# The gate and up tiles of a SwiGLU FFN multiplied in pairs by seven half products (a Strassen step) in an fp32 encoder trunk

## The reference, cut to what matters

```python
def swiglu(x, w_gate, w_up, w_down):        # x 512x1024, gate and up 1024x2816, down 2816x1024
    return (jax.nn.silu(x @ w_gate) * (x @ w_up)) @ w_down

for i in range(DEPTH):                      # 4
    ...                                     # h = mixer(x): convolution, spatial gating, short convolution, convolution
    x = layer_norm(ALPHA * x + h, ln1_g[i], ln1_b[i])
    x = layer_norm(ALPHA * x + swiglu(x, ffn_w_gate[i], ffn_w_up[i], ffn_w_down[i]), ln2_g[i], ln2_b[i])
    gate = jax.nn.sigmoid(x @ ple_w_gate[i])
    x = x + gate * rms_norm(p[i] @ ple_w_proj[i], ple_norm_g[i])
```

## Time and profile before

| | |
|---|---|
| time, three runs | 2602.64, 2599.68, 2602.08 us, median 2602.08 us |
| the profiled execution | span 2597.9 us from first to last instruction; the page gives no device time of its own for it, the median of the runs is 4.2 us above the span |
| instructions | 34084, of them 14649 matmuls |
| busy, share of the span | TensorE matmuls 99%, VectorE 55%, ScalarE 40%, GpSimd 0% |
| transfers | 239.63 MB, mean 92 GB/s |

### The profile page before, as it was taken

One profiled execution on the slowest core, in us unless ns is written; L12 is line 12 of the kernel. 1 busy time (PEld: TensorE's weight loads), 2 busy tenths in 40 slices (PEclk: granted clock), 3 DMA queues, 4 the chain that ended last, 5 costly groups with the idle time before them and its releaser, 6 DMA issues.

```text
span 2597.9 us, 34084 instructions
## 1 busy us (share of the span) xinstructions
PE 2574.2 (99%) x14649; PEld 2235.0 (86%) x14649; DVE 1421.1 (55%) x1639; ACT 1049.3 (40%) x1692; POOL 1.4 (0%) x10
## 2 busy tenths in 40 slices
PE   9999999999999999999999999999999999999999
PEld 7999888889888898888898898888898999888888
DVE  7978333277454663333784473333677977333276
ACT  6765222226233252222362253222356765222235
POOL 0000000000000000000000000000000000000000
PEclk9999999999999999999999999999999999999999
DMA  5203333324222223333232323333322113333322
GB/s 161 66 26 98 97 97 97 99 88 130 89 98 89 82 90 97 97 98 106 82 98 97 98 74 110 95 97 104 97 90 97 60 36 94 98 96 97 99 84 79
DMA packets 193290, 239.63 MB, mean 92 GB/s; under 512 B 14908, under 2 KB 139124, under 8 KB 193012
## 3 DMA queue, kind: packets, MB, share of 16 engines
q1 hardware_dynamic: 192564, 236.94, 28.8%
q10 hardware_dynamic: 576, 0.52, 0.1%
HBM read 233.21 MB, written 2.10 MB: 91 GB/s over the span
## 4 chain that ended last, share of the span: by engine, by line
PE 91%; DVE 7%; ACT 1%; issue 0%; DMA 0%; SPq 0%; DVEq 0%
PE psum L782 16%; PE psum L781 16%; PE psum L783 16%; PE psum L926 13%; PE psum L799 6%; PE psum L801 6%; PE psum L800 6%; PE psum L840 3%; PE psum L771 2%; PE psum L772 2%; PE psum L777 2%; DVE w_lo L1587 1%; DVE xf L1817 1%; DVE xf L1837 1%; DVE rstd L1829 1%; PE psum L1103 1%
## 5 line engine op out<-in xcount | busy, mean ns | idle before, releaser
L1587 DVE TENSOR_TENSOR w_lo<-raw,w_hi 128x1024 fp32r<-128x1024 f32 x431 | 517.9, 1222 | 566.2 <-ACT w_hi L1175 565.2
L1175 ACT CAST w_hi<-raw 128x1024 fp32r<-128x1024 f32 x431 | 445.1, 1048 | 673.2 <-DMA raw<-in_ffn_w_up_dram 331.8
L781 PE MATMUL psum<-a_hi,w_lo 128*128 128x512 f32 x928 | 361.4, 389 | 0.0
L783 PE MATMUL psum<-a_hi,w_hi 128*128 128x512 f32 x928 | 361.2, 389 | 0.0
L782 PE MATMUL psum<-a_lo,w_hi 128*128 128x512 f32 x896 | 348.8, 389 | 0.0
L781 PE MATMUL psum<-h_hi,w_lo 128*128 128x512 f32 x872 | 341.6, 392 | 0.0
L783 PE MATMUL psum<-h_hi,w_hi 128*128 128x512 f32 x872 | 339.6, 389 | 0.0
L782 PE MATMUL psum<-h_lo,w_hi 128*128 128x512 f32 x856 | 333.4, 389 | 0.0
L926 PE MATMUL psum<-a_hi,w_lo 128*128 128x256 f32 x1088 | 280.1, 286 | 6.7 <-DVE w_lo L1587 5.1
L926 PE MATMUL psum<-a_hi,w_hi 128*128 128x256 f32 x1088 | 276.6, 283 | 0.0
L926 PEld LDWEIGHTS psum<-a_hi,w_lo 128*128 128x128 f32 x1088 | 208.7, 192 | 8.7 <-DVE w_lo L1587 4.6
(11 more groups left out here) (299 smaller groups left out, 4053.9 us busy)
## 6 DMA issues: line engine op xcount, KB each, us to landing
raw<-in_ffn_w_gate_dram SPq DMA_DIRECT2D x176, 256.0 KB, 2.8
raw<-in_ffn_w_up_dram SPq DMA_DIRECT2D x176, 256.0 KB, 3.1
raw<-in_ffn_w_down_dram SPq DMA_DIRECT2D x176, 256.0 KB, 2.8
raw<-in_a_w_pw_dram SPq DMA_DIRECT2D x94, 256.0 KB, 2.9
raw<-in_ple_w_gate_dram SPq DMA_DIRECT2D x64, 256.0 KB, 2.7
raw<-in_b_w_in_dram SPq DMA_DIRECT2D x64, 256.0 KB, 2.9
raw<-in_c_w_in_dram SPq DMA_DIRECT2D x48, 256.0 KB, 2.9
raw<-in_b_w_out_dram SPq DMA_DIRECT2D x32, 256.0 KB, 2.7
```

Source lines behind the costliest of these rows:

```text
L781: pe.matmul(bank(grp.g, j), st_lo, mv_hi, start=(k == 0), stop=False, skip_group_check=by_tiles(grp))
L783: done = pe.matmul(bank(grp.g, j), st_hi, mv_hi, start=False, stop=(ku == last and a == UK - 1), skip_group_check=by_tiles(grp))
L1175: act.copy(hi_u[u % RING], raw_u[u % RING]).then_inc(hi_ready, 1)
L1587: dve.tensor_tensor(lo_u[u % RING], raw_u[u % RING], hi_u[u % RING].bitcast(F32), ALU.subtract)\
```

## The change

From the third group on, the FFN's gate and up product runs in a new stage, `ffn_pairs`, of 18 groups a layer. A pair is one gate tile and one up tile (128 features each). Gate and up are the two block rows, the lower and the upper half of the 1024 input features the two block columns of a 2 x 2 block matrix; tokens 0 to 255 and 256 to 511 are the two block columns of x. Seven products of half size (128 features x 512 input features x 256 tokens) take the place of eight. Each product lands in its own half bank, seven of the eight half banks of a PSUM half.

- A pair has two units. A unit holds four k-tiles of one gate and one up tile (`load_pair`), in runs of 128 columns (512 B) where before they were of 256 columns (1 KB); its bytes are as before.
- Per unit VectorE forms four sums of weight blocks (one add of 512 columns, two of 256, each on the one before), ScalarE casts three plain blocks (768 columns) and the four sums (1024), VectorE subtracts 768 and 1024 columns (`pair_hi`, `pair_lo`). Their work space is the w_hi slots and, for every third unit, other buffers: three units' worth (`work_freed`).
- Per layer four sums of x blocks are formed and split (`sum_tokens`, `sum_lo`).
- TensorE issues 7 x 2 x 3 = 42 matmuls of 256 columns a unit (`pair`).
- Behind a pair ScalarE copies one half bank (`pairs_first`), VectorE makes four additions of half banks, placed between the steps of a later unit's `pair_lo`, ScalarE takes silu in SBUF (`pairs_gate`), VectorE multiplies (`pair_product`).
- The hidden tiles of the pairs are cast and subtracted in the down projection (`hidden_split`, `hidden_lo`), since the x sums lie in their place until then. The down projection's first six casts wait until their w_hi slots are free of pair work (`hi_freed`).

```diff
+PLAIN = 2
+PAIRS = D_FF // P - 2 * PLAIN
+PAIR_UNITS = 2
+SPLIT_AT = 2 * PLAIN
+WORK = 3
...
-        stage("ffn_in", layer, DT, FT // 2)
+        stage("ffn_in", layer, DT, PLAIN)
+        stage("ffn_pairs", layer, DT, PAIRS)
...
+        def pair_slots(u):
+            s, n = pair_unit(u)
+            first = s.groups[0].unit
+            if n % WORK == 0:
+                return mean_var[:, 0:3 * HALF], tiles(h_hi, SPLIT_AT, 2), sums_lo[:, :], tiles(tmp, 4, 2)
+            slots = [(first + WORK * (n % WORK - 1) + i) % RING for i in range(WORK)]
+            return hi_u[slots[0]][:, 0:3 * HALF], hi_u[slots[1]], hi_u[slots[2]], hi_f32[slots[2]]
...
+        def work_freed(u):
+            s, n = pair_unit(u)
+            if n >= WORK:
+                return pe_done, used[u - WORK]
+            return pe_done, used[s.groups[0].unit - (RING - WORK + 1, 1)[n - 1]]
+        def hi_freed(u):
+            for s in stages:
+                if s.kind == "ffn_pairs" and 0 <= u - s.groups[-1].unit - PAIR_UNITS < RING:
+                    end = s.groups[-1].unit + PAIR_UNITS
+                    return pe_done, used[end - (2 if u - end < WORK else 1)]
+            return None
...
+            def load_pair(s, grp, ku):
+                u, f = grp.unit + ku, SPLIT_AT + grp.index
+                sp.wait_ge(*slot_freed(u))
+                dst = raw_u[u % RING].rearrange("p (i k n) -> p i k n", i=2, k=TILES)
+                for i, name in enumerate(("ffn_w_gate", "ffn_w_up")):
+                    view = ins[name][s.layer].rearrange("(k e p) n -> p e k n", e=PAIR_UNITS, p=P)
+                    sp.dma_start(dst[:, i], view[:, ku, :, f * P:(f + 1) * P])\
+                      .then_inc(raw_landed[u % RING], 16)
...
+            def pair(s, grp):
+                if grp.index == 0:
+                    pe.wait_ge(token_lo, TILES * (s.layer + 1))
+                take_half(grp.g)
+                for ku in range(PAIR_UNITS):
+                    u = grp.unit + ku
+                    pe.wait_ge(pair_x_lo, pair_count(u))
+                    pe.wait_ge(*lo_of_unit(u))
+                    x_hi, s_hi, s_lo, _ = pair_slots(u)
+                    x_lo = lo_u[u % RING][:, HALF:4 * HALF]
+                    own = lambda i: (piece(x_hi, i), piece(x_lo, i))
+                    added = lambda i: (piece(s_hi, i), piece(s_lo, i))
+                    for at, w, y in ((0, own(1), (0, 0)), (2, own(2), (1, 0)), (3, added(2), 2), (5, added(0), 0),
+                                     (6, added(1), 1), (1, added(3), (1, 1)), (4, own(0), 3)):
+                        o = piece(bank(grp.g, 0, TILES), at)
+                        for a in range(UK):
+                            k = ku + PAIR_UNITS * a
+                            w_hi_k, w_lo_k = (x[:, a * P:(a + 1) * P] for x in w)
+                            if isinstance(y, int):
+                                y_hi, y_lo = (piece(x, k) for x in token_sum(y))
+                            else:
+                                y_hi, y_lo = (hcol(tiles(x, TILES * y[0] + k), y[1]) for x in (a_hi, a_lo))
+                            first = k == 0 and at in (0, 2, 5, 6)
+                            pe.matmul(o, w_lo_k, y_hi, start=first, stop=False, skip_group_check=True)
+                            pe.matmul(o, w_hi_k, y_lo, start=False, stop=False, skip_group_check=True)
+                            done = pe.matmul(o, w_hi_k, y_hi, start=False, stop=(ku == PAIR_UNITS - 1 and a == UK - 1),
+                                             skip_group_check=True)
+                        if at == 4 if ku == 0 else at in (3, 6, 1, 4):
+                            done.then_inc(pe_done, 1)
...
+                if hi_freed(u):
+                    act.wait_ge(*hi_freed(u))
                 act.copy(hi_u[u % RING], raw_u[u % RING]).then_inc(hi_ready, 1)
             split_end = [0]
+            def pair_hi(u):
+                x_hi, s_hi, _, sums = pair_slots(u)
+                act.wait_ge(raw_landed[u % RING], 32 * (u // RING + 1))
+                if pair_unit(u)[1]:
+                    act.wait_ge(*work_freed(u))
+                act.copy(x_hi, raw_u[u % RING][:, HALF:4 * HALF]).then_inc(pair_x_hi, 1)
+                act.wait_ge(pair_sums_ready, pair_count(u))
+                act.copy(s_hi, sums).then_inc(hi_ready, 1)
+                split_end[0] = u + 1
...
+            def pairs_first(s, p):
+                act.wait_ge(pe_done, s.groups[p].end())
+                if PAIRS * s.layer + p >= 2:
+                    act.wait_ge(pair_prod, PAIRS * s.layer + p - 1)
+                act.copy(piece(pair_work(p), 1), piece(bank(s.groups[p].g, 0), 0)).then_inc(pair_first, 1)
+            def pairs_gate(s, p):
+                act.wait_ge(pair_out, PAIRS * s.layer + p + 1)
+                gate = tiles(pair_work(p), 1)
+                act.activation(gate, gate, ACT.Silu, scale=-1.0).then_inc(pair_gate, 1)
+            def ffn_in(s):
+                pairs = following(s)
+                u0 = pairs.groups[0].unit
+                split_to(u0)
+                for c in range(TILES):
+                    act.wait_ge(token_sums, TILES * s.layer + c + 1)
+                    act.copy(token_sum(c)[0], tiles(h_f32, SUM_LO + 2 * c, 2)).then_inc(token_hi, 1)
+                pair_hi(u0)
+                plain_gate(s, s.groups[0])
+                plain_hi(s, s.groups[0])
+                pair_hi(u0 + 1)
+                plain_gate(s, s.groups[1])
+                pair_hi(u0 + 2)
+                plain_hi(s, s.groups[1])
+            def ffn_pairs(s):
+                u0, units = s.groups[0].unit, PAIR_UNITS * PAIRS
+                for n in range(1, units):
+                    if n % 2 == 0:
+                        pairs_first(s, n // 2 - 1)
+                    if n + WORK - 1 < units:
+                        pair_hi(u0 + n + WORK - 1)
+                    if n % 2 == 0:
+                        pairs_gate(s, n // 2 - 1)
+                split_to(u0 + units + WORK)
+                pairs_first(s, PAIRS - 1)
+                pairs_gate(s, PAIRS - 1)
+            def hidden_split(s, ku):
+                act.wait_ge(pe_done, s.groups[0].mark)
+                act.wait_ge(pair_prod, PAIRS * s.layer + 2 * (ku - PLAIN) + 2)
+                act.copy(tiles(h_hi, 2 * ku, 2), tiles(h_f32, HL + 2 * ku, 2)).then_inc(hidden_hi, 1)
...
-                split_to(grp.unit + 9)
+                for ku in range(PLAIN, FT // 2):
+                    hidden_split(s, ku)
+                    split_to(grp.unit + ku + 2)
...
+            def pair_lo(u, between=()):
+                assert lo_end[0] == u
+                lo_end[0] = u + 1
+                x_hi, s_hi, s_lo, sums = pair_slots(u)
+                raw4 = raw_u[u % RING]
+                between = list(between) + [None] * 4
+                dve.wait_ge(raw_landed[u % RING], 32 * (u // RING + 1))
+                if pair_unit(u)[1]:
+                    dve.wait_ge(*work_freed(u))
+                own.add(dve.tensor_tensor(blocks2(piece(sums, 0, 2)), many(piece(raw4, 0), 2), blocks2(piece(raw4, 1, 2)), ALU.add))
+                step(between[0])
+                own.settle()
+                own.add(dve.tensor_tensor(piece(sums, 2), piece(raw4, 2), piece(sums, 0), ALU.add))
+                step(between[1])
+                own.settle()
+                dve.tensor_tensor(piece(sums, 3), piece(raw4, 3), piece(sums, 2), ALU.add).then_inc(pair_sums_ready, 1)
+                step(between[2])
+                dve.wait_ge(pair_sums_ready, pair_count(u))
+                dve.wait_ge(pair_x_hi, pair_count(u))
+                dve.tensor_tensor(piece(lo_u[u % RING], 1, 3), piece(raw4, 1, 3), x_hi.bitcast(F32), ALU.subtract)\
+                   .then_inc(pair_x_lo, 1)
+                step(between[3])
+                dve.wait_ge(hi_ready, u + 1)
+                dve.tensor_tensor(s_lo, sums, s_hi.bitcast(F32), ALU.subtract).then_inc(lo_ready, 1)
+            def pair_outputs(s, p):
+                grp, work = s.groups[p], pair_work(p)
+                halves = bank(grp.g, 0, TILES)
+                def up_first():
+                    dve.wait_ge(pe_done, grp.end())
+                    dve.wait_ge(pair_first, PAIRS * s.layer + p + 1)
+                    own.add(dve.tensor_tensor(every_other(work, 0), many(piece(work, 1), 2), blocks2(piece(halves, 2, 2)), ALU.add))
+                def up_second():
+                    own.settle()
+                    own.add(dve.tensor_tensor(every_other(work, 1), many(piece(work, 2), 2), blocks2(piece(halves, 5, 2)), ALU.add))
+                def up_last():
+                    own.settle()
+                    own.add(dve.tensor_tensor(piece(work, 1), piece(work, 1), piece(halves, 1), ALU.add))
+                def gate():
+                    dve.tensor_tensor(blocks2(piece(work, 2, 2)), many(piece(work, 3), 2), blocks2(piece(halves, 4, 2)), ALU.add)\
+                       .then_inc(pair_out, 1)
```

(103 more changed lines are left out.)

66 lines of the change are left out of this document (50 added, 16 removed).

## The result

The changed kernel takes 2544.54 us (median of 4 runs, 2543.58 to 2546.59) against 2602.36 us: ratio 0.9782, 95% interval 0.9768 to 0.9796, 57.8 us less. The forecast was 2554.5 with a range of 2543 to 2584; its sum without any wait was 2544.5, and that is what came out.

What follows compares the result with a forecast made beforehand. TensorE's matmul time was taken to bound the kernel, with VectorE slightly slower in the pairs after the change. -57.6 + 4 x (2.0 waiting + 0.5 late down projection) = -47.6 gave 2554.5 us, range 2543 to 2584.

Steps and rivals of the forecast that it cites:

- its sum without any wait: Whole kernel if TensorE never waits in the pairs: 2544.5 us, the lower bound of the forecast.
- TensorE's part: Pairs' matmuls: 84 halves at 0.120 us, 10.08 us a pair against 10.88 before; saves 57.6 us if TensorE never waits.
- the pairs would do less than they say: Rival, 5%: half matmuls in the pairs run slower than 0.120 us over 180 us on end; near 2602 at 0.1295.
- VectorE's part: VectorE's work per pair: 5.79 us even unit plus 4.45 odd, 10.40 with extras, 0.32 slower than TensorE's 10.08.
- some four a pair, 0.16: VectorE in the pairs: starts hanging on two semaphores cost 0.04 us more each, 0.16 us a pair.
- The lead: Entry to the pairs: VectorE finishes unit 4 at 283.7 us, TensorE wants it at 286.8, so 3.1 us early.
- 2.0 us of waiting a layer: TensorE's wait for VectorE in units 4 to 35: 16 pairs x 0.32 us, less 3.1.
- One sign that the prediction named: Pairs' outputs on VectorE some 10.1 us apart early in the stage and 10.4 late.
- The start of the down projection: Its first cast waits for the last pair unit but one, making the projection about 0.5 us a layer late.
- Other edits: ScalarE's work, moved hidden-tile casts and subtractions, PLE casts and 512 B transfers: all expected hidden, apart from 0.5 us a layer.
- The transfers: Weight loads for the pairs in 512 B runs: expected to cost nothing; rival, 2%, that they cannot feed units, from 2560 up.
- The slow side: Rival, 6%: VectorE's starts in the pairs never overlap, 11.2 us a pair, +14.4 us, 2616; decides from 11.05 us a pair.

## Why the prediction was right

- **TensorE's part** held to the digit: 0.1200 us a half matmul also over 180 us on end, 10.08 a pair, 57.6 us in all (57.8 measured). The Trainium skill's rate (TensorE: Matmul & The Clock Gate, Part 1) would have given 86 us by the prediction's estimate. This trace does not agree with it: the fixed part of 13 ns a matmul that the trace of before showed is also there after (0.1200 against 256 / 2.4 GHz = 0.1067). That the pairs would do less than they say is refuted by the same rows.
- **VectorE's part** was right in its bill, 10.24 us against 10.25 measured, with 5.79 and 4.45 against 5.78 and 4.47. What failed is the addition "some four a pair, 0.16" for starts that hang on two semaphores. L1837 waits for TensorE and for ScalarE and starts 0.60 behind its neighbour, as an independent one does. The 0.08 us that I read out of the four additions in the earlier trace rows had another cause, which was not tried. The deficit was 0.16, not 0.32.
- **The lead** was 3.3 us where 3.1 was worked out. The pairs that draw on it are 15 (unit 4 to unit 34), not 16. So the "2.0 us of waiting a layer" were 0, with 0.9 us of lead to spare at unit 34. Had the deficit been 0.32, some 1.5 (15 x 0.32 - 3.3) would have been paid; the run with one more addition, whose first up additions stand 10.57 us apart late in the stage (429.79 and 440.36), paid 4.67 in layer 0. One sign that the prediction named did not come: the outputs are not 10.1 us apart early and 10.4 late, but 10.25 from the first on (281.77 and 292.02), since VectorE runs at its own pace from there.
- **The start of the down projection**, "about 0.5 us a layer late", was 0, and it was 0 even where VectorE has no lead. In the run with one more addition the last half matmul of layer 0's pairs and the first of the down projection are 0.12 us apart, the plain spacing:

```profile
456.12 0.28 PE L1191 MATMUL psum<-h_hi,w_hi 128*128 128x256 f32 x1
456.24 0.40 PE L879 MATMUL psum<-h_hi,w_lo 128*128 128x512 f32 x1
```

The prediction let the last outputs but one begin when unit 34 is through with its slot. They need only the pair before it, and begin ahead of that moment: at 445.05 in the changed kernel, where unit 34 is through at 446.57. The first weight part of the down projection is ready at about 450.4 and wanted at 451.61.
- These two terms, 8 and 2 us, are the whole miss of 10. The mechanism was right (VectorE a little slower, a lead that covers it), and the forecast gain of 47.6 us was 10 too small because both terms were given a cost that they do not have. That the kernel came out at the very edge of its sum, with no wait at all, rests on 0.9 us of lead a layer, which the prediction did not foresee.
- **Other edits** cost nothing. The hidden tiles' subtractions run in the down projection, one beside each unit's weight part, without a wait of TensorE. The transfers landed in 3.0 and 3.3 us, 0.2 later than in the earlier trace rows, and no engine waited for them in the pairs. That the runs of 512 B are the cause is not shown, since the down projection's, whose runs are unchanged, went from 2.8 to 3.1 as well:

```profile
raw<-in_ffn_w_gate_dram SPq DMA_DIRECT2D x176, 256.0 KB, 3.0
raw<-in_ffn_w_up_dram SPq DMA_DIRECT2D x176, 256.0 KB, 3.3
raw<-in_ffn_w_down_dram SPq DMA_DIRECT2D x176, 256.0 KB, 3.1
```

- **The slow side** (no overlap of neighbours, 11.05 us a pair as the point from which it decides) did not come: L1847 starts 0.35 us after an addition that lasts 0.43. The section of the Trainium skill that the prediction quotes for it (VectorE: DVE Perf Modes, "The DRAIN you can't avoid") adds that a next instruction that is not held starts earlier, which the prediction left out; with that addition it does not contradict. The point itself was nearly met by an experiment: at 10.25 + 1.32 = 11.57 the kernel is 26 us slower than before; by the slope of 64 us for each microsecond, it would meet the kernel before at 11.17.
- A slip in the text: the product at 267.10 is that of the second group, as its row says, not of the third; the nine periods from there to the last group are right.

No run here beats the changed kernel. TensorE has no wait left in the pairs, and the run with less work on VectorE shows that easing that engine gains nothing.

## What to carry to other kernels

A Strassen step buys its eighth only as far as a half-size instruction costs half: price the smaller instruction from start to start in a stage that already has it, here 0.120 against 0.2267, and the "eighth" is 7.4%. Then bill the side engine by starts, dependent and independent ones apart, and compare its period with the main engine's. Where the side engine's is longer by little, the question is how many periods the lead at the entry covers; such a kernel has no room for one more small instruction, as 18 us for one addition of 256 columns a pair show. An instruction that stands in the wait between two dependent ones is billed only by what it adds to that wait: here one of 0.34 us was worth 0.16.

## What was not expected of the hardware

Satisfied waits cost VectorE nothing that these traces show: with two semaphores ahead of an instruction its start was still 0.60 (L1837) or 0.33 us (L1818) behind its neighbour's where both had been reached. And the starts scatter: TensorE reached the first pair at 267.68, 268.14 and 270.17 us in three executions with the same work up to there. Part of it is clock. In the profiles of the changed kernel, of the one with one more addition and of the one with an eighth product, the granted clock averages 0.79 from 237 to 245 us, just behind a wait of TensorE of 1.9 us; in the six others it is 1.00 there, behind the same wait. The wait alone does not settle whether the clock falls, and what does is not shown.
